# VectorE's order in four attentions: a job's row maxima ahead of the reciprocal sums of the job before it

## The reference, cut to what matters

```python
def softmax_attention(q, k, v, mask_or_bias):      # one head, one block of 128 queries
    s = q @ k.T * scale + mask_or_bias
    p = exp(s - max(s, axis=-1))                   # row maxima
    p = p / sum(p, axis=-1)                        # reciprocal of the row sums
    return p @ v
```

## Time and profile before

| what | value |
|---|---|
| median of the runs (lowest, highest) | 2726.37 us (2717.0, 2736.56) |
| profiled execution, its own time | 2727.66 us |
| its span | 2726.4 us |
| PE, PEld, DVE, ACT, POOL busy | 89%, 66%, 66%, 45%, 15% |
| granted TensorE clock, mean | 0.935 of full speed |
| the four attentions | about 177 to 226 us (`dil`), 232 to 261 us (`mla`), 673 to 747 us (`odd`), 1210 to 1334 us (`na`) |

### The profile page before, as it was taken

One profiled execution on the slowest core, in us unless ns is written; L12 is line 12 of the kernel. 1 busy time (PEld: TensorE's weight loads), 2 busy tenths in 40 slices (PEclk: granted clock), 3 DMA queues, 4 the chain that ended last, 5 costly groups with the idle time before them and its releaser, 6 DMA issues.

```text
span 2726.4 us, 27434 instructions
## 1 busy us (share of the span) xinstructions
PE 2437.7 (89%) x10997; PEld 1809.5 (66%) x10999; DVE 1787.2 (66%) x2013; ACT 1222.2 (45%) x1435; POOL 404.3 (15%) x467
## 2 busy tenths in 40 slices
PE   3977889876989978999989986999999999999997
PEld 2444787533568754745479755878787878787785
DVE  4564487675338863535354414888888888888886
ACT  1132543211334321112154314767676767777774
POOL 1044451122226210005312000000000000000000
PEclk9978899887589988999989997999999999999998
DMA  7630478544027880620236432999999999999994
GB/s 276 257 125 1 185 277 310 219 154 185 1 97 269 313 298 31 247 85 1 108 128 200 178 117 98 340 351 340 352 335 356 340 344 347 337 359 334 357 348 180
DMA packets 51086, 625.76 MB, mean 230 GB/s; under 512 B 8727, under 2 KB 9416, under 8 KB 11848
## 3 DMA queue, kind: packets, MB, share of 16 engines
q1 hardware_dynamic: 45216, 618.42, 60.7%
q10 hardware_dynamic: 4072, 5.40, 0.6%
q0 software_dynamic: 1664, 0.11, 0.0%
HBM read 622.85 MB, written 1.05 MB: 229 GB/s over the span
## 4 chain that ended last, share of the span: by engine, by line
PE 74%; DVE 13%; ACT 4%; DMA 4%; POOL 3%; issue 2%; ACTq 0%; DVEq 0%; SPq 0%; POOLq 0%
PE psum L1068 15%; PE psum L1070 15%; PE psum L1069 15%; DVE sbuf L684 5%; PE psum L957 4%; PE psum L984 4%; PE psum L2100 3%; DVE ring_r L1063 2%; PE psum L1101 2%; PE psum L1146 2%; PE psum L2094 2%; PE psum L2008 1%; PE psum L2574 1%; PE psum L829 1%; DMA ring<-in_t_mlp 1%
## 5 line engine op out<-in xcount | busy, mean ns | idle before, releaser
L1063 DVE TENSOR_TENSOR ring_r<-ring,sbuf_r 128x2048 fp32r<-128x2048 f32 (+1 forms) x309 | 564.1, 1829 | 159.5 <-ACT sbuf_r L1054 156.7
L1069 PE MATMUL psum<-ring_r,sc_r 128*128 128x512 f32 x1688 | 665.0, 394 | 0.0
L1054 ACT CAST sbuf_r<-ring 128x2048 fp32r<-128x2048 f32 (+1 forms) x309 | 467.8, 1519 | 400.9 <-PE psum L1070 282.1
L1063 DVE TENSOR_TENSOR ring_r<-ring,sc_r 128x2048 fp32r<-128x2048 f32 (+1 forms) x221 | 448.9, 2036 | 148.3 <-ACT sc_r L1054 148.1
L1054 ACT CAST sc_r<-ring 128x2048 fp32r<-128x2048 f32 (+1 forms) x221 | 375.3, 1701 | 218.6 <-PE psum L1070 205.8
L1068 PE MATMUL psum<-sbuf_r,sc_r 128*128 128x512 f32 (+1 forms) x1236 | 464.0, 375 | 7.0 <-DVE sc L2421 3.1
L1070 PE MATMUL psum<-sbuf_r,sc_r 128*128 128x512 f32 x948 | 374.4, 395 | 0.0
L684 DVE SCALAR_TENSOR_TENSOR sbuf<-ring,sbuf 128x512 f32<-128x512 f32 x416 | 332.7, 806 | 51.8 <-DMA sbuf<-in_ada_b 17.6
L1069 PEld LDWEIGHTS psum<-ring_r,sc_r 128*128 128x128 f32 x1688 | 316.9, 188 | 73.2 <-issue 3.1
L1068 PE MATMUL psum<-sc_r 128*128 128x512 f32 x740 | 296.9, 401 | 0.9 <-DVE sc_r L2606 0.9
L1070 PE MATMUL psum<-sc_r 128*128 128x512 f32 x740 | 289.8, 392 | 0.0
(11 more groups left out here) (293 smaller groups left out, 2865.3 us busy)
## 6 DMA issues: line engine op xcount, KB each, us to landing
ring<-in_t_moe SPq DMA_DIRECT2D x168, 2048.0 KB, 7.9
ring<-in_t_ada SPq DMA_DIRECT2D x48, 2048.0 KB, 9.0
ring<-in_t_mlp SPq DMA_DIRECT2D x32, 2048.0 KB, 8.4
ring<-in_t_win SPq DMA_DIRECT2D x17, 2048.0 KB, 9.7
ring<-in_t_ffn SPq DMA_DIRECT2D x23, 1024.0 KB, 5.2
ring<-in_t_out SPq DMA_DIRECT2D x7, 2048.0 KB, 8.1
ring<-in_t_ffn SPq DMA_DIRECT2D x5, 2048.0 KB, 8.8
ring<-in_t_bias SPq DMA_DIRECT2D x2, 2048.0 KB, 9.9
```

Of the source, the lines that this page charges most:

```text
L1054: p.act.e.copy(p.r(hi), src).then_inc(*p.sig("high", st.tag, n))
L1063: p.dve.e.tensor_tensor(p.r(src), src, p.r(hi), ALU.subtract).then_inc(*p.sig("lowp", st.tag, n))
L1069: e.matmul(out, l[0], r[1], start=False, stop=False)
```

## The change

`dve_softmax` is split in two. `dve_max` waits for the scores, adds the bias where there is one, and takes the row maxima of job i. `dve_over` waits for the exponential of its job, and takes the reciprocal and, in the second differential jobs, the two operations behind it. A round of VectorE now calls `dve_max` for job i and then `dve_over` for job i - 1, before its evictions. The last job's `dve_over` falls into the round after the last. All other engines' lists stay as they are, and no instruction is added or removed.

```diff
-def dve_softmax(p, A, i):
+def dve_max(p, A, i):
 
     e = p.dve.e
     j = A.jobs[i]
     sp = A.span(p, A.s_banks[i % len(A.s_banks)])
-    nd, sm = p.ND[:, i % 8:i % 8 + 1], p.SUMS[:, i % 8:i % 8 + 1]
     p.dve.wait_ge(*p.at("score", A.tag, i))
...
-    e.tensor_reduce(nd, sp[:, 0:j.cols], X_AXIS, ALU.max, negate=True).then_inc(*p.sig("max", A.tag, i))
+    e.tensor_reduce(p.ND[:, i % 8:i % 8 + 1], sp[:, 0:j.cols], X_AXIS, ALU.max, negate=True).then_inc(
+        *p.sig("max", A.tag, i))
+
+
+def dve_over(p, A, i):
+
+    e = p.dve.e
+    j = A.jobs[i]
+    sm = p.SUMS[:, i % 8:i % 8 + 1]
     p.dve.wait_ge(*p.at("exp", A.tag, i))
     e.reciprocal(sm, sm).then_inc(*p.sig("over", A.tag, i))
     if j.kind == "second":
...
-def dve_round(p, A, one, two, end):
+def dve_round(p, A, i, one, two, end):
+
     if one is not None:
-        dve_softmax(p, A, one)
+        dve_max(p, A, one)
+    if 1 <= i <= len(A.jobs):
+        dve_over(p, A, i - 1)
     if two is not None:
         put_turned(p, p.dve, "D", A, two)
     if end is not None:
```

More of the change, by code:

```diff
@@ L1524, in dve_even @@
     for i, one, two, end in steps(p.dil):
-        dve_round(p, p.dil, one, two, end)
+        dve_round(p, p.dil, i, one, two, end)
         for m in range(3 * i, 3 * i + 3):
@@ L1538, in dve_even @@
     dve_turn(p, "mk", p.KT, 8, [0, 1], rows=96)
-    for _, one, two, end in steps(p.mla):
-        dve_round(p, p.mla, one, two, end)
+    for i, one, two, end in steps(p.mla):
+        dve_round(p, p.mla, i, one, two, end)
     dve_products(p, 8, 11)
@@ L1888, in dve_odd @@
     for i, one, two, end in steps(p.odd):
-        dve_round(p, p.odd, one, two, end)
+        dve_round(p, p.odd, i, one, two, end)
         if i == 3:
@@ L2321, in dve_mix @@
     for i, one, two, end in steps(p.na):
-        dve_round(p, p.na, one, two, end)
+        dve_round(p, p.na, i, one, two, end)
         if i % 4 == 3 and i < 32:
```

## The result

The changed kernel takes 2774.93 us, the median of four runs (2761.37 to 2786.9), against 2730.82 us for four runs of the kernel before: ratio 1.0163, 95% interval 1.0107 to 1.0218. It is slower by about 44 us. The forecast was 2760 us with a range of 2740 to 2782.

What follows compares the result with a forecast made beforehand. The attentions were taken to be bound by TensorE's idle time and lag, not VectorE's. 19 (`dil`) + 0.3 (`mla`) - 0.5 (`odd`) + 13.8 (`na`) = 32.6 us on 2727.66 gave 2760 us, range 2740 to 2782.

Steps and rivals of the forecast that it cites:

- What bounds the kernel: All four attentions: they matter only by how long TensorE stands still or lags; it is idle 32.6 us together.
- The signs that were named: Trace: VectorE idle moves in `dil`, `dil` some 19 us longer, `mla` and `odd` within 2 us, `na` convolution 4 us later.
- `dil`, +19: `dil`, depth 1: scalings wait for the next job's maxima and TensorE's transposes for them, growing job by job; +14 to +23 us.
- the choice between the levels: `dil`: +16.8 us with TensorE at the high clock level where possible, about +21 with low-level stretches; +19 was taken.
- `mla`, +0.3: `mla`, depth 2: the later scaling ends about when ScalarE's eviction does, so values hardly move; -1 to +3 us.
- `odd`, -0.5: `odd`, depth 3: scalings are wanted two rounds late, so all in time; the turn comes about 0.5 us earlier; -2 to +2.
- `na`, +13.8: `na`, depth 2: late scalings around convolution steps, +2.35 us four times, +1.0 three times, 1.3 at the ends; +5 to +18.
- The clock falls too: Rival: some 30 us of `na` work moves to the low clock level, adding some 25 us, 2785 us; chance 0.17.
- Only `dil` pays: Rival: in `na` TensorE's full rounds leave slack, so scalings are ready in time; 2746 us; chance 0.20.
- Faster: Rival: VectorE's wait held up maxima, exponentials and scores, so removing it gains at most 32.6 us, to 2695; chance 0.04.

Runs made afterwards that it cites:

- `dil` alone: The changed order in the `dil` attention only, the other three in the old order, against the kernel before: ratio 1.0069, `dil` 67.25 us.
- the filled kernel: The change in `na` only, plus useless matmuls in TensorE's waits before transposes of jobs 4, 8, ..., 28, against the kernel before: ratio 1.0065, `na` 141.8 us.
- `na` alone: The changed order in the `na` attention only, the others in the old order, against the kernel before: ratio 1.0088, `na` 148.6 us.
- jobs 4m + 3 put back: The change in `na` only, but the eight jobs whose round has a convolution step keep the old order, against the kernel before: ratio 1.0045, `na` 140.6 us.
- depth 3: The change in `na` only, with TensorE's transposes and values one round later (2 raised to 3), against the kernel before: ratio 1.0051, `na` 135.1 us.
- the filling matmuls of 660.30: All attentions in the old order, plus 32 useless matmuls in TensorE's idle time ahead of `odd`, against the kernel before: ratio 1.0003, `odd` 71.7 us.

## Why the prediction was right, and where it was off

**What bounds the kernel** was read rightly: it is how long TensorE waits or lags, not VectorE's idle time. VectorE's 62.7 us went to 3.4 and brought the 1.8 us of `odd`, no more. Its share of the windows was read a little low: 25 of 49 us and 68 of 124 are 51% and 55%, not half or less; nothing hung on it. The signs that were named came, but for `mla`, whose length changed by 2.6 us with the clock: VectorE's idle time in `dil` rose from 6.8 to 15.4 us before the maxima and from none to 9.3 before its evictions, and in `na` GpSimd's first convolution operation starts 8.9 us behind the matmuls of step 1 where it was 5.0.

**`dil`, +19, measured 17.5** in the trace of after, 18.9 in that of `dil` alone, and 0.69% (19 us) by the runs. The working job by job held: scaling 0 forecast at 184.3 and seen at 184.11, scaling 3 at 205.3 (207.6 less 2.2 and 0.1) and 204.88, scaling 4 between 211.4 and 213.8 and at 212.29, scaling 5 at 223.5 and 223.81, scaling 6 at 232.0 and 232.27. For the trace of after the choice between the levels was a little too dark: transposes 3 ran at the high level and scores 5 behind them partly (2.63 us, for 2.93 at the low level), so the end was 0.7 over the high level's sum and 3.5 under the low one's. In the run of `dil` alone transposes 3 and scores 5 took 1.54 and 2.93 us, and 18.9 us is nearly the forecast. By the section "HAM oscillation" of the page "TensorE: Matmul & The Clock Gate" of the Trainium skill alone it would have been 21; that section's own case has waits of about 3 to 5 us. The trace agrees for transposes 5 (1.54 us behind a wait of 6.17, with the work ahead of it at the high level). It doesn't for transposes 3, which took 0.88 us behind a wait of 3.24; in the run of `dil` alone the same transposes took 1.54 behind 3.25. Transposes 1 tell nothing, for the scores ahead of their wait were at the low level already (1.65 us for 0.93).

**`mla`, +0.3**: +0.6 at equal clock, and the wait moved from the ScalarE eviction to GpSimd as worked out. The -2.6 of the traces is a difference in the clock that the old order shows among its own traces too.

**`odd`, -0.5**: -1.8. The turn came 0.7 us earlier, as said. The rest is at the stage's end, where TensorE comes to the high level earlier and the last values take 0.83 us and not 1.51, and wasn't foreseen.

**`na`, +13.8, measured 24.8**: this is the step of the sum that was mis-sized. Its waits are right: forecast 0.9 and about 2.4 us in steps 0, 1, 4, 5 and 1.0 in steps 2, 3, 6, seen 0.82, 2.29 and 1.33, 1.33 and 1.08 (where 0.31 of waiting for ScalarE went away), and 12.9 us in sum by the filled kernel for 13.8. But the working took the transposes and values behind each wait at their old durations. Seven products with the values went to the low level, with some transposes and scores next to them, and that is 11.9 us more (15.0 less the 3.1 of before). The row that would have told it was among those quoted: the values of 1261.37, 3.57 us for 1.91 behind a wait of 0.31. It was put into a rival (*The clock falls too*, 30 us of work at the low level, 2785, chance 0.17) and not into the sum. That rival was half true: in `na` the clock did cost 12 us, in the other stages nothing beyond what the sum had. The median, 2774.93, lies between the two cases, and nearer to the rival's 2785 than to 2760.

**The sum.** 32.6 us forecast and 33.7 seen in the profiled pair agree by luck: `na` was 11 us too low, and the traces' pair happened to differ by 2.6 in `mla` and by 3.9 us outside the stages (-5.7 + 1.8) in favour of the kernel after. Against the medians' 44 the forecast is 11 short, which is `na`; the median itself lies 15 over the forecast, for the kernel before took 2730.82 in these runs and 2727.66 in the sum.

**The other rivals.** *Only `dil` pays* fell with the run of `na` alone, 1.0088. Its argument, that TensorE's full rounds give slack, is true for half of the jobs. *Faster* fell: the exponentials came earlier, but the earlier trace rows's loop didn't shorten, for scores, maxima and exponential are still in a row in it.

## What to carry to other kernels

A wait on an engine that isn't the bound is worth what stands behind it, not its length: moving a short instruction past "a wait of 0.7 us" moved it past the next job's scores, and every engine behind it in order paid. Before an order is changed, ask for each consumer how much other work the bounding engine has between the new start and its need: with depth 1 none, in `na` 1.7 us for every fourth job and, by adding up the rows, over 3.5 for those that have the values or the convolution in between. And price a new wait of TensorE at its length plus what the matmuls behind it take at the low level; in `na` that nearly doubled the bill.

## What the runs showed of the hardware

- What a wait does to the clock doesn't follow from its length alone. In `na` of the changed kernel the seven waits of 1.08 to 2.29 us before the transposes of jobs 4, 8, ..., 28 were all followed by slow values (2.83 to 3.62 us), and so were the same seven in the run of `na` alone and seven of 1.34 in that with jobs 4m + 3 put back; the four of 0.82 were followed by none. But at depth 3 waits of 1.64 us right before the values were followed by 1.91 us twice and by slow values twice. Waits of 0.3 to 0.65 us were sometimes followed by slow values, sometimes not. In `dil` the transposes behind a wait of 3.24 us kept the high level in one trace (0.88 us), and behind 3.25 in another they didn't (1.54). The same stretch of `na` with the long waits filled had no slow values at all.
- `odd` at 0.50 to 0.52 with TensorE busy for 92% of it doesn't keep a high level that it starts with: 2.2 us. The Trainium skill's page "TensorE: Matmul & The Clock Gate", Part 4, would put it down to transposes; in that trace no transposes ran between the filling matmuls of 660.30 and the fall, so here they can't be the only reason.
- The stretch between `mla` and `odd`, which no kernel changed, differs by up to 12 us between traces (405.3 to 417.6); why is open. `mla` with its turns in the old order differs by up to 3.2, and there it is the level at which the heads happen to run. A stage's gain under 3 us needs its rows at equal clock, not its length.
